# Conv input projection x in the wide form: cross half through ScalarE, main half through VectorE, four PSUM banks in turn

## The reference, cut to what matters

```
h = rms_norm(x, g_mix)
proj = h @ w_in
b_a, c_a, x_a, u_p, q, k, v, ga, gp, gt = split(proj)
u = c_a * x_a
y = depthwise conv of u over the tokens, 3 taps, padding 1
y_a = (b_a * y) @ w_a_out
y_p = multiscale pooling of u_p; y_t = windowed attention of q, k, v
x = x + (sigmoid(ga) * y_a + sigmoid(gp) * y_p + sigmoid(gt) * y_t) @ w_o
x = x + ffn(rms_norm(x, g_ffn))
```

## Time and profile before

| what | value |
|---|---|
| median of three runs | 1316.2 us (1315.92 to 1316.9) |
| profiled execution: time, span | 1316.9 us, 1315.1 us |
| PE busy | 1293.2 us (98% of the span) |
| PE weight loads busy | 1122.3 us (85%) |
| VectorE busy | 1047.3 us (80%) |
| ScalarE busy | 716.0 us (54%) |
| granted TensorE clock | 0.999 of full speed |
| DMA | 262.64 MB, mean 200 GB/s |

### The profile page before, as it was taken

One profiled execution on the slowest core, in us unless ns is written; L12 is line 12 of the kernel. 1 busy time (PEld: TensorE's weight loads), 2 busy tenths in 40 slices (PEclk: granted clock), 3 DMA queues, 4 the chain that ended last, 5 costly groups with the idle time before them and its releaser, 6 DMA issues.

```text
span 1315.1 us, 19827 instructions
## 1 busy us (share of the span) xinstructions
PE 1293.2 (98%) x7552; PEld 1122.3 (85%) x7552; DVE 1047.3 (80%) x1734; ACT 716.0 (54%) x1150; POOL 55.6 (4%) x106
## 2 busy tenths in 40 slices
PE   7999999999999999999999999999999999999998
PEld 5999898888888888998898888888879887888887
DVE  4887677877778786887687777788888898698888
ACT  5565555455454455555545464454458567655554
POOL 1111000000000000000000000000010000000000
PEclk9999999999999999999999999999999999999999
DMA  9866446664777745454446756778634514355551
GB/s 298 256 202 198 159 160 226 229 239 151 270 252 287 251 179 192 160 170 155 156 159 230 270 186 217 269 280 293 232 123 147 222 65 163 110 197 191 192 190 65
DMA packets 43000, 262.64 MB, mean 200 GB/s; under 512 B 5645, under 2 KB 6413, under 8 KB 15646
## 3 DMA queue, kind: packets, MB, share of 16 engines
q1 hardware_dynamic: 32688, 227.28, 48.9%
q0 software_dynamic: 10128, 34.06, 8.2%
q10 hardware_dynamic: 94, 0.07, 0.0%
HBM read 259.81 MB, written 1.58 MB: 199 GB/s over the span
## 4 chain that ended last, share of the span: by engine, by line
PE 93%; DVE 4%; ACT 2%; issue 1%; DMA 0%; SPq 0%; DVEq 0%; ACTq 0%
PE psum L789 21%; PE psum L836 17%; PE psum L910 12%; PE psum L795 11%; PE psum L843 9%; PE psum L769 8%; PE psum L775 4%; PE psum L969 1%; PE psum L992 1%; PE psum L1153 1%; PE psum L981 1%; DVE split L2068 1%; PE psum L928 1%; PE psum L734 1%; PE psum L807 0%
## 5 line engine op out<-in xcount | busy, mean ns | idle before, releaser
L2068 DVE TENSOR_TENSOR split<-ring,split 128x1024 fp32r<-128x1024 f32 x406 | 479.6, 1220 | 59.4 <-ACT split L1482 58.2
L1482 ACT CAST split<-ring 128x1024 fp32r<-128x1024 f32 x405 | 405.9, 1051 | 168.7 <-PE psum L910 68.4
L789 PE MATMUL psum<-h,split 128*128 128x512 f32 x1216 | 290.1, 390 | 0.0
L789 PEld LDWEIGHTS psum<-h,split 128*128 128x128 f32 x1216 | 225.0, 188 | 44.8
L910 PE MATMUL psum<-split,feed 128*128 128x512 f32 x792 | 185.3, 390 | 0.0
L910 PEld LDWEIGHTS psum<-split,feed 128*128 128x128 f32 x792 | 146.7, 188 | 29.4 <-DVE split L2068 0.2
L836 PE MATMUL psum<-split,h 128*128 128x512 f32 x664 | 163.9, 393 | 0.2
L795 PEld LDWEIGHTS psum<-h,split 128*128 128x128 f32 x1216 | 156.2, 191 | 6.1
L795 PE MATMUL psum<-h,split 128*128 128x256 f32 x1216 | 158.0, 283 | 0.0
L836 PEld LDWEIGHTS psum<-split,h 128*128 128x128 f32 x664 | 122.2, 188 | 25.4 <-issue 0.6
L769 PE MATMUL psum<-h,split 128*128 128x256 f32 x896 | 112.3, 283 | 0.0
(11 more groups left out here) (350 smaller groups left out, 1344.3 us busy)
## 6 DMA issues: line engine op xcount, KB each, us to landing
ring<-stream SPq DMA_DIRECT2D x213, 1024.0 KB, 4.9
arena<-ada POOLq DMA_DIRECT2D x48, 512.0 KB, 5.7
arena<-bias_by_distance POOLq DMA_DIRECT2D x32, 96.0 KB, 4.8
gain<-norm_rows POOLq DMA_DIRECT2D x4, 512.0 KB, 5.4
x<-x_in SPq DMA_DIRECT2D x2, 512.0 KB, 4.9
ring<-stream SPq DMA_DIRECT2D x2, 512.0 KB, 7.3
arena<-norm_rows POOLq DMA_DIRECT2D x2, 512.0 KB, 5.7
gain<-mod_rows POOLq DMA_DIRECT2D x2, 512.0 KB, 4.0
```

Of the source, the lines that this page charges most:

```text
L789: pe.matmul(bank[b + m].rearrange("p (a t) -> p a t", a=2), w[0][:, k, m * P:(m + 1) * P], h[:, :, k, :], start=k == 0, stop=False)
L1482: act.copy(split_of(x)[:, 0, n], ring[:, AT[x] % RING, n]).then_inc(wh_ready, 1)
L2068: return dve.tensor_tensor(out_, value, high.bitcast(F32), ALU.subtract)
```

## The change

x is computed by `project_both`, into two banks. Which banks are used alternates with j: c in 0 and 1, x in 2 and 3, b in bank 0 for even j; c in 2 and 3, x in 0 and 1, b in bank 2 for odd j. PE therefore waits before x(j) for the product of b(j-1), before b(j) for the sum of c(j), before c(j+1) for the sum of x(j), and before ga0 for the sum of x3. ScalarE gets a copy of x's cross part into `tmp` (after the low part of `feed` of j-1, which reads `tmp`); VectorE gets an addition of the main part into `tmp`, and its product into `upad` reads `tmp` and `stage` from SBUF.

```diff
-        CONV_BANK = {"c": 0, "x": 2, "b": 3}
+        def conv_bank(name, j):
+            return ({"c": 0, "x": 2, "b": 0}, {"c": 2, "x": 0, "b": 2})[j % 2][name]
...
                         if (name, j) == ("ga", 0):
-                            pe.wait_ge(c_summed, l * 4 + 4)
+                            pe.wait_ge(x_summed, l * 4 + 4)
...
                         else:
-                            pe.wait_ge(c_summed, l * 4 + j)
-                    elif name in ("x", "b"):
-                        pe.wait_ge(*release((name, j - 1) if j else ("kd", CONV_BANK[name] - 2), l))
+                            pe.wait_ge(x_summed, l * 4 + j)
+                    elif name == "x":
+                        pe.wait_ge(*release(("b", j - 1) if j else ("kd", 1), l))
+                    elif name == "b":
+                        pe.wait_ge(c_summed, l * 4 + j + 1)
...
-                    elif name == "c":
-                        mm = project_both(CONV_BANK[name], c)
-                    elif name in ("x", "b"):
-                        mm = project(CONV_BANK[name], c, h)
+                    elif name in ("c", "x"):
+                        mm = project_both(conv_bank(name, j), c)
+                    elif name == "b":
+                        mm = project(conv_bank(name, j), c, h)
...
-                        act.copy(stage, cross_part(CONV_BANK[name])).then_inc(act_evac, 1)
+                        act.copy(stage, cross_part(conv_bank(name, j))).then_inc(act_evac, 1)
+                    elif name == "x":
+                        act.wait_ge(job_done, l * NJOBS + k + 1)
+                        if j >= 1:
+                            act.wait_ge(yin_ready, l * 4 + j)
+                        act.copy(tmp, cross_part(conv_bank(name, j))).then_inc(x_cross, 1)
...
                     if name == "x":
 
+                        dve.wait_ge(x_cross, l * 4 + j + 1)
+                        dve.tensor_tensor(tmp, main_part(conv_bank(name, j)), tmp, ALU.add).then_inc(x_summed, 1)
                         dve.wait_ge(c_summed, l * 4 + j + 1)
-                        dve.tensor_tensor(upad[:, :, 1:1 + T], halves(CONV_BANK[name]), stage, ALU.mult).then_inc(dve_evac, 1)
+                        dve.wait_ge(x_summed, l * 4 + j + 1)
+                        dve.tensor_tensor(upad[:, :, 1:1 + T], tmp, stage, ALU.mult).then_inc(dve_evac, 1)
```

More of the change, by code:

```diff
@@ L463, in bass_stack_kernel @@
         c_summed = sem("c_summed")
+        x_cross = sem("x_cross")
+        x_summed = sem("x_summed")
         ao_split = sem("ao_split")
@@ L2243, in _ @@
                         dve.wait_ge(act_evac, l * len(ACT_JOBS) + act_count(("c", j)))
-                        dve.tensor_tensor(stage, main_part(CONV_BANK[name]), stage, ALU.add).then_inc(c_summed, 1)
+                        dve.tensor_tensor(stage, main_part(conv_bank(name, j)), stage, ALU.add).then_inc(c_summed, 1)
                     if name == "x":
+                        dve.wait_ge(x_cross, l * 4 + j + 1)
+                        dve.tensor_tensor(tmp, main_part(conv_bank(name, j)), tmp, ALU.add).then_inc(x_summed, 1)
                         dve.wait_ge(c_summed, l * 4 + j + 1)
-                        dve.tensor_tensor(upad[:, :, 1:1 + T], halves(CONV_BANK[name]), stage, ALU.mult).then_inc(dve_evac, 1)
+                        dve.wait_ge(x_summed, l * 4 + j + 1)
+                        dve.tensor_tensor(upad[:, :, 1:1 + T], tmp, stage, ALU.mult).then_inc(dve_evac, 1)
                         dve.wait_ge(dve_evac, l * len(DVE_JOBS) + dve_count(("x", j)))
@@ L2262, in _ @@
                             dve.wait_ge(yin_ready, l * 4 + j)
-                        dve.tensor_tensor(tmp, halves(CONV_BANK[name]), y1, ALU.mult).then_inc(dve_evac, 1)
+                        dve.tensor_tensor(tmp, halves(conv_bank(name, j)), y1, ALU.mult).then_inc(dve_evac, 1)
                         next_low((l, name, j))
```

## The result

The changed kernel takes 1320.09 us (median of 8, 1319.39 to 1320.61) against 1316.14 us before (median of 8): 1.0031 times as long, 95% interval 1.0022 to 1.0040, about +4 us. It is slower, by a little more than can be told from no change. The predicted time, 1318.5, is 1.6 us short and on the other side of that bound; the time lies inside the range.

A forecast was written before the change was run, and what follows sets the result against it. PE issue was taken to bound the conv stage of both layers. With PE's savings included, layer 0's +1.91 and layer 1's +0.36 sum to +2.3 us: 1318.5 us on the median, range 1314.4 to 1320.8.

The forecast's parts named there:

- What bounds, and PE's saving: Conv stage of both layers: bound by PE issue; eight wide x chunks save 0.18 us each, 1.4 us in all.
- The added wait and its place: x's copy queues behind ScalarE's exponentials (1.09 us), delaying VectorE; PE's scores wait about 1.6, 0.8, then 0.3, 0.5 us.
- PE's new bank waits cost nothing: Waits before x(j), b(j), c(j+1) cost nothing: each has a 5.6 us chunk of PE work between.
- The hand-offs: At each x: copy to sum about 0.03 us, sum to product 0.73 us.
- d: Extra time of copy, add, product, release at each x; 5d in all, over 0.2% slower from d = 0.07.
- rival 2: Hand-offs at each x cost more than counted; d = 0.3 gives +4.2 us, 1320.4 us; chance 0.3.
- x0 of layer 0: Add follows upad's clearing at about 60.70, product at 61.43 instead of 60.87: 0.56 us late.
- the sum of 2.3: Whole kernel: 1.91 us from layer 0 plus 0.36 us from layer 1, +2.3 us.
- Rival 1: Room at PE's gates is larger than counted, nothing reaches PE: -1.4 us, 1314.8 us; chance 0.2, partial cases included.
- S: Delay of x(j)'s product against its old time, reaching the softmax input's release in full; 1.96 us at x1, layer 0.
- The chance of slower: Whole kernel over 0.2% slower than before: 0.37, against 0.6 for within 0.2% and 0.03 for faster.
- The two rules weighed: Skill's matmul gap formula (0.3 us saved in all) and 58 + N cycles (moved product 0.065 us cheaper); trace preferred.

The follow-up runs named there:

- the chain in the kernel before: Kernel before, x narrow on the old banks, plus ScalarE's copy of x's bank and one extra VectorE operation (maximum of bank and copy): 1320.63 us.
- fewer waits: Changed kernel without VectorE's wait for c's sum ahead of x's product and, except at x0, its wait for x's end ahead of the copy wait: 1319.00 us.
- mended kernel: Changed kernel with x0 of layer 0 narrow, softmax input straight behind b's product, two implied waits out: 1314.47 us, 1315.01 us in a second set.
- b wide: The mended kernel with b computed wide as well, its cross part copied through tmp and added by VectorE: 1312.70 us.

## Why the prediction was right or wrong

**What bounds, and PE's saving: right.** With the copy and the sum left out the kernel is 0.8 to 1.2 us faster than before, where 1.4 less 0.6 was due; in the stretch it is 0.85, and x1's own chunk is 0.19 shorter.

**The added wait and its place: right.** The copy starts 0.09 us behind the exponentials at x1 and x2. The idle column shows 0.27, 1.55 and 0.69 us in layer 0, and 0.71 at c2 of layer 1; there is none later, though after ga0 of layer 1 the gate opens only just in time (609.22, scores at 609.28). Forecast were 0.1, 1.6, 0.8, and 0.3 and 0.5. The column is a lower bound. From start to start, corrected, with 0.18 saved per x, the stalls are 0.45 (c1: 71.86 against 71.81, less x0's 0.59), 1.90 and 0.96 in layer 0. In layer 1 they are 0.35 at c1 (550.14 against 547.68) and 0.94 at c2. The one at c1 stands at the weight load ahead of the scores and not at their product:

```profile
550.13 0.54 PEld L972 LDWEIGHTS psum<-k_pair,q_first 128*128 128x128 f32 x4 [0.35 <-DVE small L2205]
```

That is 4.6 us in all, where the forecast's own numbers make 3.7 (2.09 + 3 x 0.18 and 0.72 + 2 x 0.18).

**"PE's new bank waits cost nothing": wrong.** This is the step that failed in its mechanism. It named x(j), b(j) and c(j+1) and gave each a chunk of room. But x0 waits for the second key transpose, whose bank the conv stage did not need before b0. Its low part ends after c0 does in layer 0. In the trace of before:

```profile
53.41 1.29 DVE L2068 TENSOR_TENSOR k_pair<-psum,k_pair 128x512 fp32r<-128x512 f32 x2
54.16 4.09 PE L769 MATMUL psum<-h,split 128*128 128x256 f32 x32
```

The low part ends at 54.70, and x0's products start at 54.16. Cost: 0.59 us, once, since in layer 1 the first scores already wait for the same low part. Its end against the end of c0 was the row to look up.

**The hand-offs: mis-sized.** Copy to sum and sum to product were taken as 0.03 and 0.73; they measure 0.10 and 0.79, d = 0.13 of rival 2, from the second wait on an instruction. At x0 only the second counts, since the clearing hides the first. That is 0.07 + 0.13 + 0.13 = 0.33 us before c3 of layer 0 and 0.20 before c2 of layer 1.

**x0 of layer 0: mis-sized.** After the clearing of upad the sum starts 0.48 us late (60.47 to 60.95), 0.44 more than the forecast's 0.04 (60.70 behind a clearing that would end at 60.66). It is the same with the chain in the kernel before, and with fewer waits (0.48 each), and absent in layer 1 (the clearing ends at 538.46, the sum starts at 538.51). In the mended kernel, whose first sum is that of x1, the sum starts 0.03 behind the copy, so it is not simply the first sum of the program; what it is stays open.

Together: forecast 1.91 for layer 0, plus 0.59, 0.33 and 0.44, makes 3.27; the corrected traces show 3.10 at layer 1's first scores. Layer 1: 0.36 plus 0.20 makes 0.56; shown 0.59. So the sum of 2.3 should have been 3.8, and the medians show 3.95.

**The rivals.** Rival 1 is out: PE waits. Its condition was also tighter than stated: with PE due at 90.29 and the release at 90.08 plus 0.05 to the start, S at x1 had to be below 0.16, not 0.3. Rival 2 named a mechanism that is there, and its threshold, d = 0.07 at each x, was passed. But it is a third of the 1.5 us missed; the rest is x0's bank and x0's late sum, which I had not named. At d = 0.13 rival 2 alone gives 2.3 + 0.65, 1319.2. That the measured time lies inside the range is therefore partly luck: the upper end was drawn for a d of 0.3, and it happened to cover two terms that the sum did not have. The chance of slower, 0.37, was too low for a forecast 0.3 us below the bound with five places at which a small error is added up.

**The two rules weighed.** By the gap formula of the Trainium skill (TensorE: Matmul & The Clock Gate, Back-to-back issue gap) the eight chunks would save 0.3 us, less than x0's bank costs. The kernel without copy and sum is faster all the same, by 0.85 us in the stretch, and x1's chunk is 0.19 us shorter, so the trace's 0.18 a chunk stands. For the product from SBUF the trace of after has 0.69 us, as from PSUM. The Trainium skill (VectorE: DVE Perf Modes, the section on the TRN2 errata) has two formulas, of which (N + 151)/0.96, 0.69 us for N = 512, holds here; 58 + N cycles, 0.59 us, does not.

## What to carry to other kernels

When an engine that is not the bottleneck gets a longer loop, ask not for its idle share (VectorE had 20%) but for the loop's length against the bottleneck's cycle, and for the room at the gate that comes last in each cycle: 0.57 us here, found by setting a semaphore's release against its waiter's start. Put the operation that opens such a gate first in the helper engine's order; that alone turned a loss of 4 us into nothing. With x0 of layer 0 left narrow and the implied waits out it also made room for the wide form to pay, 3.4 us with b included. And don't count a saving on the bottleneck in full ahead of a gate that opens late: here about 0.5 of the 1.44 us seems to have been waited away there. And when banks are reassigned, check the first turn of the loop by itself: its wait goes to whoever had the bank before the loop.

## What the runs showed of the hardware

A VectorE instruction with two semaphore waits starts 0.07 us later than with one, even if one of the two has long been satisfied: 0.79 to 0.80 against 0.72 from start to start of dependent operations (changed kernel against fewer waits). And the load of x at the start takes between 5.02 us (b wide) and 6.33 us (fewer waits) over the twelve traces, from 5.20 to 6.02 in after and before alone, a difference as large as what four chunks of this change save. The fourth q chunk starts between 41.49 and 42.95, so two traces are to be aligned at an instruction ahead of the change before their times are compared.
